# Gathering a prompt's 64 rows as 128 half rows before they are transposed for the experts

## The reference, cut to what matters

```python
def expert_choice_ffn(x, w_router, w_gate, w_up, w_down):
    b, s, d = x.shape
    T = b * s
    cap = CAPACITY_FACTOR * T // N_EXPERTS
    h = x.reshape(T, d)
    aff = jax.nn.softmax((h @ w_router).astype(jnp.float32), axis=-1)
    gate_vals, tok_idx = lax.top_k(aff.T, cap)
    xg = h[tok_idx]
    hid = jax.nn.silu(jnp.einsum('ecd,edf->ecf', xg, w_gate)) * jnp.einsum('ecd,edf->ecf', xg, w_up)
    out = jnp.einsum('ecf,efd->ecd', hid, w_down) * gate_vals[..., None].astype(x.dtype)
    y = jnp.zeros_like(h).at[tok_idx.reshape(-1)].add(out.reshape(-1, d))
    return y.reshape(b, s, d)
```

## Time and profile before

| | |
|---|---|
| time, median of 3 runs | 3386.62 us (3384.24 to 3389.15) |
| span of the profiled execution | 3382.4 us |
| median less that span | 4.2 us |
| PE busy | 3333.9 us, 99% of the span |
| PEld busy | 3096.4 us, 92% |
| DVE busy | 2296.4 us, 68% |
| ACT busy | 1886.4 us, 56% |
| POOL busy | 396.3 us, 12% |
| mean granted TensorE clock | 0.995 of full speed |

### The profile page before, as it was taken

How to read it: one execution, slowest core, us unless ns; L and a number is a source line. 1 busy time by engine, 2 the same in 40 slices (tenths; PEclk the granted TensorE clock), 3 DMA queues, 4 the chain that set the end, 5 groups by cost and what they waited for, 6 DMA issues and landing times.

```text
span 3382.4 us, 59690 instructions
## 1 busy us (share of the span) xinstructions
PE 3333.9 (99%) x20423; PEld 3096.4 (92%) x20423; DVE 2296.4 (68%) x3928; ACT 1886.4 (56%) x3235; POOL 396.3 (12%) x397
## 2 busy tenths in 40 slices
PE   9999999999899999999999999999999999999997
PEld 7889899889798999999898999999898989999896
DVE  6522267688876767767676767667676767667687
ACT  4222367642265656656565656656565656556576
POOL 0011166432000000000000000000000000000013
PEclk9999999999999999999999999999999999999999
DMA  5334446254477777777777777777777787777786
GB/s 196 118 114 156 120 98 166 91 208 159 172 243 243 233 241 235 236 236 238 230 240 244 229 246 235 236 237 237 236 236 237 236 244 235 238 235 227 236 295 231
DMA packets 250869, 720.76 MB, mean 213 GB/s; under 512 B 55649, under 2 KB 71073, under 8 KB 250369
## 3 DMA queue, kind: packets, MB, share of 16 engines
q1 hardware_dynamic: 233568, 660.54, 59.7%
q0 software_dynamic: 16688, 57.69, 6.1%
q10 hardware_dynamic: 432, 0.10, 0.0%
HBM read 656.14 MB, written 66.16 MB: 214 GB/s over the span
## 4 chain that ended last, share of the span: by engine, by line
PE 73%; DMA 0%; POOL 0%; issue 0%; DVE 0%; POOLq 0%; ACT 0%
PE moe_gu L2468 33%; PE moe_gu L2469 15%; PE moe_dns L2481 5%; PE moe_dns L2483 5%; PE moe_dnp L2486 5%; PE moe_dnp L2487 5%; PE moe_dns L2482 5%; PE moe_dns L2454 0%; PE moe_dns L2455 0%; PE moe_gu L130 0%; DMA moe_xg_s<-tmp_h,moe_grow_s 0%; POOL moe_rstd L2439 0%; DMA moe_guv<-in_ident 0%; POOLq L2208 0%; DVE moe_base_s L2773 0%
## 5 line engine op out<-in xcount | busy, mean ns | idle before, releaser
L2468 PE MATMUL moe_gu<-moe_xgT,moe_whi 128*128 128x384 f32 x5632 | 1619.2, 361 | 0.0
L2697 DVE TENSOR_TENSOR moe_wlo<-moe_raw,moe_whi 128x1024 fp32r<-128x1024 f32 x1056 | 1292.5, 1224 | 457.9 <-ACT moe_whi L2583 456.0
L2469 PE MATMUL moe_gu<-moe_xgT,moe_wlo 128*128 128x192 f32 x5632 | 1408.2, 250 | 0.0
L2583 ACT CAST moe_whi<-moe_raw 128x1024 fp32r<-128x1024 f32 x1056 | 1105.8, 1047 | 386.8 <-PE moe_dnp L2487 378.5
L2469 PEld LDWEIGHTS moe_gu<-moe_xgT,moe_wlo 128*128 128x128 f32 x5632 | 1075.7, 191 | 0.6
L2468 PEld LDWEIGHTS moe_gu<-moe_xgT,moe_whi 128*128 128x128 f32 x5632 | 1057.3, 188 | 0.8 <-issue 0.2
L2481 PE MATMUL moe_dns<-moe_whi,moe_hid 128*128 128x512 f32 x704 | 275.9, 392 | 0.0
L2486 PE MATMUL moe_dnp<-moe_whi,moe_hid 128*128 128x512 f32 x704 | 275.6, 392 | 0.0
L2483 PE MATMUL moe_dns<-moe_wlo,moe_hid 128*128 128x512 f32 x704 | 275.6, 391 | 0.0
L2487 PE MATMUL moe_dnp<-moe_wlo,moe_hid 128*128 128x512 f32 x704 | 275.5, 391 | 0.0
L2482 PE MATMUL moe_dns<-moe_whi,moe_hid 128*128 128x512 f32 x704 | 275.4, 391 | 0.0
(11 more groups left out here) (419 smaller groups left out, 4385.1 us busy)
## 6 DMA issues: line engine op xcount, KB each, us to landing
moe_raw<-in_w_ffn SPq DMA_DIRECT2D x1056, 512.0 KB, 4.1
res_early<-in_w_in SPq DMA_DIRECT2D x10, 1024.0 KB, 5.7
tmp_qkT<-res_raw POOLq DMA_DIRECT2D x24, 256.0 KB, 2.8
res_early<-tmp_qkT SPq DMA_DIRECT2D x16, 384.0 KB, 6.7
res_raw<-tmp_qkT SPq DMA_DIRECT2D x16, 384.0 KB, 7.0
res_early<-tmp_xbc SPq DMA_DIRECT2D x12, 512.0 KB, 3.7
res_early<-in_x SPq DMA_DIRECT2D x12, 512.0 KB, 4.9
tmp_h<-res_early SPq DMA_DIRECT2D x12, 512.0 KB, 2.6
```

Source lines behind the costliest of these rows:

```text
L2468: pe.matmul(out[:, a, 0:2 * CAP], whi[c][:, j, :], x, start=(j == 0), stop=False)
L2469: mm = pe.matmul(out[:, a, 0:CAP], wlo[c][:, j, :], x[:, 0:CAP], start=False, stop=(j == KD - 1))
L2583: act.copy(whi[c][:], raw[c][:]).then_inc(hi_done, 1)
L2697: dve.tensor_tensor(wlo[c][:], raw[c][:], whi[c][:].bitcast(F32), ALU.subtract).then_inc(lo_done, 1)
```

## The change

The prompt's rows are read from `h` seen as 3072 half rows of 512: half row 2r+a is half a of row r. `xg[1]` becomes 128 x 512, with the 64 first halves on partitions 0 to 63 and the 64 second halves on 64 to 127. One transpose of a 128-column block of it yields block b of the first halves and block b of the second halves, which are the blocks b and b+4 of the rows. So a call of `fill_tokens` now turns blocks b and b+4 in three transposes, and the products take the blocks in the order 0, 4, 1, 5, ... The list of half rows (`half_rows`, 2r and 2r+1) is made once in `choose`; the prompt's whole rows, which the scatter needs, are got back from it by halving. The zeroing of `xg[1]`'s lower half falls away.

```diff
-        grow = [m.sb("grow_s", [NS, 1], U32), m.sb("grow_p", [NP_, 1], U32)]
+        grow = [m.sb("grow_s", [NS, 1], U32), m.sb("grow_p", [2 * NP_, 1], U32)]
+        half_rows = m.sb("half_rows", [2 * NP_, EXPERTS], U32)
+        sources, listed = [dram["h"], dram["h"].rearrange("t (a d) -> (t a) d", a=2)], [res["rows"][0], half_rows]
...
-        xg = [m.sb("xg_s", [NS, D]), m.sb("xg_p", [P, D])]
+        xg = [m.sb("xg_s", [NS, D]), m.sb("xg_p", [2 * NP_, D // 2])]
...
-                    pool.indirect_dma_start(xg[i][0:CAPS[1 - i], :], None, dram["h"], bass.IndirectOffsetOnAxis(ap=grow[i][:], axis=0)).then_inc(xg_in, 16)
+                    pool.indirect_dma_start(xg[i][:], None, sources[i], bass.IndirectOffsetOnAxis(ap=grow[i][:], axis=0)).then_inc(xg_in, 16)
...
-                    pool.tensor_copy(grow[i][:], res["rows"][i][:, bass.ds(e, 1)]).then_inc(grow_ready, 1)
+                    pool.tensor_copy(grow[i][:], listed[i][:, bass.ds(e, 1)]).then_inc(grow_ready, 1)
...
-            pool.memset(xg[1][NP_:, :], 0.0).then_inc(xg_pad, 1)
-            pool.wait_ge(xg_pad, 1)
...
                 for j in range(2):
-                    k = 2 * b + j
-                    pe.transpose(turned(e, b)[:, j, 0:P], xg[0][:, P * k:P * k + P], ident)
-                    mm = pe.transpose(turned(e, b)[:, j, P:2 * P], xg[1][:, P * k:P * k + P], ident)
+                    k = b + KD // 2 * j
+                    pe.transpose(turned(e, b)[:, j, 0:NS], xg[0][:, P * k:P * k + P], ident)
+                mm = pe.transpose(turned(e, b)[:, :, NS:CAP], xg[1][:, P * b:P * b + P], ident)
                 mm.then_inc(tok_fill, 1)
...
-                    for j in range(KD):
-                        if e == FIRST and i == 0 and a == 0 and j % 2 == 0:
-                            pe.wait_ge(tok_done, j // 2 + 1)
+                    for n in range(KD):
+                        if e == FIRST and i == 0 and a == 0 and n % 2 == 0:
+                            pe.wait_ge(tok_done, n // 2 + 1)
+                        j = n // 2 + KD // 2 * (n % 2)
...
-            pe.transpose(lists[0:NP_, 5, :], rowp, one).then_inc(lists_mm, 1)
+            pe.transpose(lists[:, 5, :], rowp, one).then_inc(lists_mm, 1)
...
-                act.copy(xgT[q][:, 2 * b:2 * b + 2, 0:CAP], turned(e, b)[:, :, 0:CAP]).then_inc(tok_hi, 1)
+                act.copy(xgT[q][:, b::KD // 2, 0:CAP], turned(e, b)[:, :, 0:CAP]).then_inc(tok_hi, 1)
...
-                dve.tensor_copy(rowp, idx[PR:PR + EXPERTS, 8 * ROUNDS:]).then_inc(lists_ready, 1)
+                for a in range(2):
+                    dve.tensor_scalar(rowp[:, NP_ * a:NP_ * a + NP_], idx[PR:PR + EXPERTS, 8 * ROUNDS:], 2.0, float(a), ALU.mult, ALU.add).then_inc(lists_ready, 1)
                 dve.wait_ge(lists_mm, 1)
-                dve.tensor_copy(res["rows"][1][:], lists[0:NP_, 5, :]).then_inc(choice, 1)
-                dve.tensor_copy(grow[1][:], lists[0:NP_, 5, FIRST:FIRST + 1]).then_inc(grow_ready, 1)
+                dve.tensor_copy(half_rows[:], lists[:, 5, :]).then_inc(choice, 1)
+                dve.tensor_copy(grow[1][:], lists[:, 5, FIRST:FIRST + 1]).then_inc(grow_ready, 1)
+                dve.tensor_scalar(res["rows"][1][:], lists[0:NP_, 5, :], 0.5, None, ALU.mult).then_inc(choice, 1)
...
-                dve.tensor_tensor(xgT[q][:, 2 * b:2 * b + 2, CAP:2 * CAP], turned(e, b)[:, :, 0:CAP],
-                                  xgT[q][:, 2 * b:2 * b + 2, 0:CAP].bitcast(F32), ALU.subtract).then_inc(tok_done, 1)
+                dve.tensor_tensor(xgT[q][:, b::KD // 2, CAP:2 * CAP], turned(e, b)[:, :, 0:CAP],
+                                  xgT[q][:, b::KD // 2, 0:CAP].bitcast(F32), ALU.subtract).then_inc(tok_done, 1)
```

More of the change, by code:

```diff
@@ L2256, in stage_experts @@
         valb, rowa, rowb = (og[0][0:EXPERTS, NS * i:NS * i + NS] for i in range(2, 5))
-        valp, rowp = (og[0][0:EXPERTS, NS * 5 + NP_ * i:NS * 5 + NP_ * i + NP_] for i in range(2))
-        tok = og[0][:, NS * 6:NS * 6 + 4 * EXPERTS].rearrange("p (n e) -> p n e", n=4)
-        first, diff, best = (og[0][:, NS * 7 + EXPERTS * i:NS * 7 + EXPERTS * i + EXPERTS] for i in range(3))
+        valp, rowp = og[0][0:EXPERTS, NS * 5:NS * 5 + NP_], og[0][0:EXPERTS, NS * 6:NS * 6 + 2 * NP_]
+        tok = og[0][:, NS * 7:NS * 7 + 4 * EXPERTS].rearrange("p (n e) -> p n e", n=4)
+        first, diff, best = (og[0][:, NS * 7 + EXPERTS * i:NS * 7 + EXPERTS * i + EXPERTS] for i in range(4, 7))
         warm = og[1][:, 0:1]
@@ L2282, in stage_experts @@
         gather_issued = m.sem("gather_issued")
-        xg_pad = m.sem("xg_pad")
         tok_fill = m.sem("tok_fill")
@@ L2463, in gate_up @@
                     pe.wait_ge(lo_done, BUFS + GR * e + 2 * k + a + 1)
-                    for j in range(KD):
-                        if e == FIRST and i == 0 and a == 0 and j % 2 == 0:
-                            pe.wait_ge(tok_done, j // 2 + 1)
+                    for n in range(KD):
+                        if e == FIRST and i == 0 and a == 0 and n % 2 == 0:
+                            pe.wait_ge(tok_done, n // 2 + 1)
+                        j = n // 2 + KD // 2 * (n % 2)
                         x = xgT[q][:, j, :]
-                        pe.matmul(out[:, a, 0:2 * CAP], whi[c][:, j, :], x, start=(j == 0), stop=False)
-                        mm = pe.matmul(out[:, a, 0:CAP], wlo[c][:, j, :], x[:, 0:CAP], start=False, stop=(j == KD - 1))
+                        pe.matmul(out[:, a, 0:2 * CAP], whi[c][:, j, :], x, start=(n == 0), stop=False)
+                        mm = pe.matmul(out[:, a, 0:CAP], wlo[c][:, j, :], x[:, 0:CAP], start=False, stop=(n == KD - 1))
                     mm.then_inc(gran_mm, 1)
@@ L2528, in _ @@
             turn_over(pe, gu[0][:, 0, :], identr[:], same, SPARE_LISTS)
-            pe.wait_ge(lists_ready, 5)
+            pe.wait_ge(lists_ready, 6)
             one = ident[0:EXPERTS, 0:EXPERTS]
@@ L2533, in _ @@
             pe.transpose(lists[0:NP_, 4, :], valp, one)
-            pe.transpose(lists[0:NP_, 5, :], rowp, one).then_inc(lists_mm, 1)
+            pe.transpose(lists[:, 5, :], rowp, one).then_inc(lists_mm, 1)
             turn_over(pe, gu[0][:, 0, :], identr[:], same, SPARE_TOKENS)
-            pe.wait_ge(xg_pad, 1)
             pe.wait_ge(xg_in, 32)
@@ L2682, in choose @@
                 dve.tensor_tensor(diff, tok[:, 1, :], tok[:, 3, :], ALU.subtract).then_inc(choice, 1)
-                dve.wait_ge(choice, 6)
+                dve.wait_ge(choice, 7)
                 dve.tensor_scalar(res["gates"][0][:], best, 1.0 / ALPHA, None, ALU.mult).then_inc(choice, 1)
                 dve.tensor_tensor(diff, diff, first, ALU.mult).then_inc(choice, 1)
-                dve.wait_ge(choice, 8)
+                dve.wait_ge(choice, 9)
                 dve.tensor_tensor(res["rows"][0][:], diff, tok[:, 3, :], ALU.add).then_inc(choice, 1)
-                dve.wait_ge(choice, 9)
+                dve.wait_ge(choice, 10)
                 dve.tensor_copy(grow[0][:], res["rows"][0][:, FIRST:FIRST + 1]).then_inc(grow_ready, 1)
```

2 lines of the change are left out of this document (1 added, 1 removed).

## The result

The changed kernel takes **3366.44 us** (median of 6 runs, 3358.90 to 3370.23) beside 3386.29 us for the kernel before (6 runs, 3384.24 to 3389.15). The ratio is 0.9937 with a 95% interval of 0.9927 to 0.9947: 0.63% faster. The prediction was 3382.0 with a range from 3378.0 to 3386.0, so the time lies outside, on the fast side. Some 20 us went where 4.6 were forecast.

A forecast was written before the change was run, and what follows sets the result against it. TensorE was taken to bound the expert stage. Fifteen experts gain 4.7 us and the part ahead of the first loses 0.1, so 3386.62 - 4.6 = 3382.0 us, range 3378.0 to 3386.0.

The forecast's parts named there:

- TensorE bounds the stage, and a transpose costs 0.109 us: Expert stage: PE is never idle, so 60 transposes removed at 0.109 us each save 6.5 us if unhindered.
- The rival that took them for the price: Turns: each removed transpose saves its whole 0.273 us, 16.4 us in all, giving 3370 us; chance 0.02.
- A new wait ahead of call 3: Second half of each turn: call 3's weight load waits for DVE's second subtraction, 0.17 us late, 0.12 net.
- The gain of 0.31 us an expert: Each turn: four transposes at 0.109 us less 0.12 us of waiting; fifteen experts gain 4.7 us.
- The two-piece write costs nothing: Prompt's transposes in the turns: writing two pieces of 64 keeps them 0.109 us apart, at no added cost.
- DVE's subtraction keeps its 0.55 us: DVE's subtraction of a pair in the turns: only the distance between its two runs grows, so its length stays 0.55 us.
- the slow rival: Turns: the wider step slows DVE's subtraction from 0.55 to 1.37 us, costing 20 us, 3406.6 us; chance 0.04.
- Ahead of the first expert 0.1 us slower: Before the expert stage: list transpose 0.05, gather issue 0.1 and packets 0.1, less 0.11 gained; between 0.1 faster and 1.2 slower.
- Costs that I take at nothing inside the loop: Expert loop: split writes, ACT's copy, DVE's subtraction, block order, POOL's gathers and weight loads, all priced at nothing.
- The products read the same blocks in another order, at no cost: Products in the expert loop: the changed order of blocks was priced at nothing.

The follow-up runs named there:

- the run that holds the change alone: The changed kernel with the tile `half_rows` made last, so `xgT` and `hid` lie 2048 bytes from their places before: 3380.33 us, ratio 0.9984.
- the tile alone: The kernel before plus an unused 64-byte tile behind `grow`, with all 16 transposes kept in each turn: 3363.32 us, ratio 0.9934.
- the run with the later half: The changed kernel with calls 2 and 3 of a turn one step later, except in the turn for the second expert: 3360.44 us, ratio 0.9925.
- the one with `xgT` moved: The kernel before with 64 unused bytes ahead of the `xgT` tiles and 64 behind, which also moved `hid` by 128: 3389.45 us, ratio 1.0014.

## Why the prediction was wrong, and where it was right

The part that was worked out held; the part that was not priced outweighed it four times.

- **TensorE bounds the stage, and a transpose costs 0.109 us.** Right. The first half of a turn, which has no wait, went from 0.852 to 0.634 us in the starts, which is two transposes of 0.109. The 0.273 us of the earlier trace rows are the length of one and not its price. The rival that took them for the price gave 3370, the nearest to the measured time of all the cases, by a mechanism that is refuted: the time alone would have confirmed it.
- **A new wait ahead of call 3, 0.05 us behind DVE's second subtraction, in every turn.** Right in place, size and count. The gain of 0.31 us an expert was 0.32 in the run that holds the change alone, and 15 x 0.31 = 4.7 us was 4.7 in its stage. Its ratio, 0.9984, is 5.4 us.
- **The two-piece write costs nothing.** Right, by the same 0.634 us: the first half of a turn shrank by just what two transposes cost, so the split ones in it cost what the others do. Their own length is that of the earlier trace rows:

```profile
L2454 PE MATMUL moe_dns<-moe_identr,moe_xg_p x62: 272/273/273, 923.9 to 3057.7; 128*128 128x128 f32 x62
```

- **DVE's subtraction keeps its 0.55 us.** Right, so the slow rival falls:

```profile
L2720 DVE TENSOR_TENSOR moe_xgT<-moe_dns,moe_xgT x62: 542/550/557, 924.7 to 3062.1; 128x384 fp32r<-128x384 f32 x62
```

- **Ahead of the first expert 0.1 us slower.** Not confirmed, and too small to be told from one profiled execution a kernel. The way from the first spare matmul to the first gate product was 22.99 us after and 23.28 before; over all the kernels run it was 21.5 to 23.0 with the new code and 22.0 to 23.7 with the old. That is rather faster than slower. PE waits no longer for the first rows than in the earlier trace rows, so twice as many indices cost nothing that can be seen.

```profile
PE moe_dns L2453 <- DMA moe_xg_s<-tmp_h,moe_grow_s: 1.5, 1, 1.5
```

- **The step that failed** is in "Costs that I take at nothing inside the loop": "The products read the same blocks in another order, at no cost". The order is indeed free. But they are the same blocks only by name: the new tile and the narrower `xg[1]` moved `xgT` and `hid` against the weights, from a distance of 192 to 0 modulo 256, and that took 2.2 ns off each pair and 2.3 off each down product, 20 us in all. I went through every instruction that the diff changes and priced none of its allocations. No rival covered a change in the 14784 matmuls (5632 pairs and 3520 down products) that the diff leaves as they are, so the range was too narrow at its lower end.

The two effects, 20.2 us (the tile alone) and 4.7 (the list last), add up to 24.9; the stage gained 22.5. The rest is a slower rhythm of the pairs that appears only in some steps of the changed kernel. Expert 1, two gate products that stand 12 pairs apart:

```profile
1176.22 0.36 PE L2468 MATMUL moe_gu<-moe_xgT,moe_whi 128*128 128x384 f32 x1
...
1179.70 0.36 PE L2468 MATMUL moe_gu<-moe_xgT,moe_whi 128*128 128x384 f32 x1
```

(1179.70 - 1176.22) / 12 = 0.290 us. Expert 1 runs so from its third step on and takes 153.2 us where its neighbours take 151.4, and so does the step between a turn's halves in the experts from 3 to 14: 12 x 16 x 5.5 ns = 1.1 us, with the 1.8 of expert 1 some 2.8. Some 0.5 comes back, since the wait in those twelve turns is 0.04 us shorter (0.70 us for their second half instead of 0.74). In the run with the later half the two steps between the halves have it, and the next pair of calls ends it; the kernel before with 64 bytes more doesn't have it at all, the one with `xgT` moved has it in one step of every third expert. It was seen only where `xgT` lies at distance 0: the two kernels with the later half and 384 or 128 bytes more have the same turns at distance 128 and not one such step. The run with the blocks from 0 to 7 has it, so the order does not bring it on. What does, at distance 0, stays open.

**Was there a sign in the trace of before?** One. The spare matmuls ahead of the experts (L130) have the 512 columns of a down product, and from the twenty-third on they start 0.2267 us apart at the full clock, where a down product takes 0.2291. (The nine gaps ahead of that, from 899.8 to 901.9 us and already at a granted clock of 1.00, are 0.231 on average; why they are wider is not shown.) They load and stream the same tile, `identr`, so their distance is 0. Two prices for one shape were there to be asked about.

## What to carry to other kernels

Here a new tile and a narrower one moved every tile of the stage that is made behind them by 1984 bytes, and that was worth some 20 us. So for a diff that adds, drops or resizes a tile, list the starts of the operands of the hot instructions before and after, as one lists the instructions. When untouched instructions change their spacing, look for what they share (here two operands' places) before explaining the time by what was edited, and test it with a tile that nobody uses; a measured time close to a rival's is no evidence for its mechanism. Of the kernels run here the best combine the four fewer transposes, the later half and a distance of 0: 3359.46 and 3360.44 us, 0.75% under before. Most of that is the distance: the kernel before with 64 unused bytes has 3363.32 us.

## What the hardware showed that I had not expected

The rate of these float32r products went with the distance modulo 256 bytes between the tile that is loaded as weights and the one that is streamed: 0.2268 to 0.2335 us for the same 512 columns, 3% between the best and the worst of the five distances run, and 0.2845 to 0.2867 for a pair of 384 and 192. For the down product each of the five has one spacing, to 0.2 ns; a pair has two at 64, and at 0 it falls at times into 0.290. This holds at a granted clock of 1.00 and with no instruction edited: an unused tile of 64 bytes alone took the down product from 0.2290 to 0.2268 us and the pair from 0.2867 to 0.2844, and with the weights moved along, the 0.2291 and 0.2867 stayed. What ties the spacing to the distance no run shows; only the dependence is measured.
